# A decoder layer's first normalised rows: norm weights spread over 128 rows, squares and tile splits moved between engines

## The reference

```
h = rms_norm(x, ffn1_norm);  x = x + 0.5 * ((silu(h @ w1) * (h @ w3)) @ w2)
h = rms_norm(x, mix_norm);   x = x + concat(attention(h), ssd(h)) @ w_out
h = rms_norm(x, ffn2_norm);  x = x + 0.5 * ((silu(h @ w1) * (h @ w3)) @ w2)
out = rms_norm(x, final_norm)

rms_norm(x, w) = x * rsqrt(mean(x * x, last axis) + 1e-6) * w
```

## Time and profile before

| | us |
|---|---|
| three runs | 558.83, 558.90, 559.13; median 558.9 |
| the profiled execution | 558.88 |
| its span, first to last instruction | 557.1 |
| TensorE busy | 542.9 (97%) |
| VectorE busy | 436.1 (78%) |
| ScalarE busy | 333.2 (60%) |
| GpSimd busy | 63.9 (11%) |

### The profile page before, as it was taken

One profiled execution on the slowest core, in us unless ns is written; L12 is line 12 of the kernel. 1 busy time (PEld: TensorE's weight loads), 2 busy tenths in 40 slices (PEclk: granted clock), 3 DMA queues, 4 the chain that ended last, 5 costly groups with the idle time before them and its releaser, 6 DMA issues.

```text
span 557.1 us, 9770 instructions
## 1 busy us (share of the span) xinstructions
PE 542.9 (97%) x3670; PEld 494.9 (89%) x3670; DVE 436.1 (78%) x659; ACT 333.2 (60%) x539; POOL 63.9 (11%) x97
## 2 busy tenths in 40 slices
PE   8999999999999989999999999999999999999994
PEld 5999899999999879998889678889999999999993
DVE  4899898888887884877766666589898988888845
ACT  6757566555654565857675874376566556556533
POOL 2003000000000420512431002000000000000015
PEclk9999999999999999999999999999999999999998
DMA  9867955545664357555324235345575566655302
GB/s 269 291 227 233 322 190 189 167 175 186 226 226 151 91 158 229 167 188 176 128 78 151 75 82 167 131 154 169 198 251 201 178 208 226 226 161 182 108 1 75
DMA packets 69359, 97.65 MB, mean 175 GB/s; under 512 B 1862, under 2 KB 55298, under 8 KB 69331
## 3 DMA queue, kind: packets, MB, share of 16 engines
q1 hardware_dynamic: 68336, 94.55, 52.1%
q0 software_dynamic: 848, 2.47, 1.5%
q10 hardware_dynamic: 146, 0.27, 0.1%
HBM read 96.23 MB, written 1.05 MB: 175 GB/s over the span
## 4 chain that ended last, share of the span: by engine, by line
PE 81%; DVE 8%; ACT 3%; DMA 3%; issue 2%; POOL 1%; SPq 0%; POOLq 0%; DVEq 0%; ACTq 0%
PE bank L1575 25%; PE bank L1577 25%; PE bank L1576 25%; DMA raw<-in_ffn_w 3%; DVE w_lo L1048 2%; PE bank L1716 1%; ACT decay L924 1%; DVE x L1065 1%; ACT w_hi L602 1%; POOL rstd L472 1%; PE bank L1881 1%; PE bank L1882 1%; PE bank L1868 1%; DVE normed L1457 1%; PE bank L1880 0%
## 5 line engine op out<-in xcount | busy, mean ns | idle before, releaser
L1575 PE MATMUL bank<-hT_hi,w_hi 128*128 128x256 f32 x736 | 208.7, 284 | 0.2 <-DVE tok_rows L1216 0.2
L1576 PE MATMUL bank<-hT_lo,w_hi 128*128 128x256 f32 x736 | 208.0, 283 | 0.0
L1577 PE MATMUL bank<-hT_hi,w_lo 128*128 128x256 f32 x736 | 208.0, 283 | 0.0
L1048 DVE TENSOR_TENSOR w_lo<-raw,w_hi 128x1024 fp32r<-128x1024 f32 x128 | 158.4, 1240 | 28.5 <-ACT w_hi L602 28.0
L602 ACT ACTIVATE w_hi<-raw 128x1024 fp32r<-128x1024 f32 x128 | 134.1, 1055 | 43.4 <-PE bank L1577 24.7
L1575 PEld LDWEIGHTS bank<-hT_hi,w_hi 128*128 128x128 f32 x736 | 140.8, 191 | 3.3 <-DVE tok_rows L1216 1.4
L1576 PEld LDWEIGHTS bank<-hT_lo,w_hi 128*128 128x128 f32 x736 | 140.8, 191 | 1.6
L1577 PEld LDWEIGHTS bank<-hT_hi,w_lo 128*128 128x128 f32 x736 | 140.9, 191 | 0.0
L1575 PE MATMUL bank<-w_hi,hT_hi 128*128 128x512 f32 (+1 forms) x192 | 70.1, 365 | 2.0 <-DVE w_lo L1082 1.0
L1577 PE MATMUL bank<-w_hi,hT_lo 128*128 128x512 f32 (+1 forms) x192 | 68.1, 355 | 0.0
L1576 PE MATMUL bank<-w_lo,hT_hi 128*128 128x512 f32 (+1 forms) x192 | 68.0, 354 | 0.0
(11 more groups left out here) (217 smaller groups left out, 810.4 us busy)
## 6 DMA issues: line engine op xcount, KB each, us to landing
raw<-in_ffn_w SPq DMA_DIRECT2D x54, 1024.0 KB, 5.4
raw<-in_w_in SPq DMA_DIRECT2D x16, 1024.0 KB, 5.5
tok_rows<-in_ffn_w SPq DMA_DIRECT2D x10, 1024.0 KB, 5.3
raw<-in_w_out SPq DMA_DIRECT2D x6, 1024.0 KB, 4.9
raw<-in_ffn_w SPq DMA_DIRECT2D x8, 256.0 KB, 5.3
x<-in_x SPq DMA_DIRECT2D x4, 256.0 KB, 3.9
out_x<-normed SPq DMA_DIRECT2D x3, 256.0 KB, 2.3
norm_w<-in_mix_norm POOLq DMA_DIRECT2D x1, 512.0 KB, 5.4
```

The source lines that it names most:

```text
L1048: dve.tensor_tensor(lo, src, hi, ALU.subtract).then_inc(half_ready, 1)
L1575: pe.matmul(dst, lhs[0], rhs[0], start=start, stop=False, skip_group_check=True)
L1576: pe.matmul(dst, lhs[0], rhs[1], start=False, stop=False, skip_group_check=True)
L1577: return pe.matmul(dst, lhs[1], rhs[0], start=False, stop=stop, skip_group_check=True)
```

## The change

The identity's load moves from SP's queue to ScalarE's, ahead of the norm load. `norm_rows` and `ones_rows` take the place of the single rows: 128 partitions, of which all but the first are zero. VectorE clears `norm_rows` (128x1024), and ScalarE's load of the norm weights waits for that (`rows_cleared`). GpSimd clears the 128x128 of ones and then sets its first row. There are three warm-up matmuls instead of two. Of the first row tile ScalarE squares the left half and VectorE the right half, by a multiply with a reduction that also adds EPS; GpSimd adds the two and takes the power. ScalarE scales the left half before it rounds the first weights, and weight roundings stand between the two copies of the transposed banks. VectorE makes all low parts of the first tiles; GpSimd's subtraction and `low_ready` are gone. The diff's core:

```diff
-        norm_row = norm_w[0:1, 0, :]
-        ones_row = mix_w[0:1, D:D + P]
+        norm_rows = norm_w[:, 0, :]
+        ones_rows = mix_w[:, D:D + P]
...
# SP
-            sp.dma_start(cst[:, C_ID:C_ID + P], consts[:, C_ID:C_ID + P]).then_inc(ident_loaded, 16)
...
# GpSimd
-            pool.memset(ones_row, 1.0).then_inc(ones_ready, 1)
+            step(pool.memset(ones_rows, 0.0))
+            pool.memset(ones_rows[0:1, :], 1.0).then_inc(ones_ready, 1)
...
-                pool.wait_ge(mean_ready, 2 * n + t + 1)
+                pool.wait_ge(mean_ready, 2 * n + t)
...
-            row_rstd(0, 0)
-
-            slot = ffn_half(0, 0, 0, 0)[1]
-            pool.wait_ge(hi_ready, 1)
-            pool.tensor_tensor(rows_part(w_lo[:, slot, :], 1), rows_src(0, 0, 1),
-                               rows_part(w_hi[:, slot, :].bitcast(f32), 1), ALU.subtract).then_inc(low_ready, 1)
+            pool.wait_ge(sq_ready, 2)
+            pool.tensor_tensor(mean_sq[:, 0:1], sumsq[:, 0, 0:1], sumsq[:, 1, 0:1], ALU.add).then_inc(left_mean_ready, 1)
+            pool.wait_ge(left_mean_ready, 1)
+            pool.tensor_tensor(rstd[:, 0:1], mean_sq[:, 0:1], minus_half[:, :], ALU.pow).then_inc(rstd_ready, 1)
             row_rstd(0, 1)
...
# ScalarE
-            act.dma_start(norm_row, norms[0].rearrange("(a d) -> a d", a=1)).then_inc(norm_loaded[0], 16)
-            for c in range(2):
-                act.wait_ge(x_loaded[c], 16)
-                square_x(0, 0, c)
+            act.dma_start(cst[:, C_ID:C_ID + P], consts[:, C_ID:C_ID + P]).then_inc(ident_loaded, 16)
+            act.wait_ge(rows_cleared, 1)
+            act.dma_start(norm_rows[0:1, :], norms[0].rearrange("(a d) -> a d", a=1)).then_inc(norm_loaded[0], 16)
+            act.wait_ge(x_loaded[0], 16)
+            square_x(0, 0, 0)
+            first_scale(0, 0)
             rows_hi(0, 0, 0)
-            first_scale(0, 0)
+            hT_hi_part(1, T_BANKS[0], 0, 0)
             rows_hi(0, 1, 0)
-            norm_hi(0, 0)
+            hT_hi_part(2, T_BANKS[1], 4, 0)
             rows_hi(0, 0, 1)
             rows_hi(0, 1, 1)
...
# VectorE
-            for c in range(2):
-                dve.wait_ge(x_loaded[c], 16)
+            right = slice(512, 1024)
+            dve.memset(norm_rows, 0.0).then_inc(rows_cleared, 1)
+            dve.wait_ge(x_loaded[1], 16)
+            dve.tensor_tensor_reduce(z_silu[:, 0, right], x[:, 0, right], x[:, 0, right], 1.0 / D, EPS,
+                                     ALU.mult, ALU.add, sumsq[:, 1, 0:1]).then_inc(sq_ready, 1)
+            dve.wait_ge(x_loaded[0], 16)
             first_weigh(0, 0)
-            rows_lo(0, 0, 0).then_inc(top_ready, 1)
             dve.wait_ge(norm_spread, 2)
             dve.wait_ge(rstd_ready, 1)
-            right = slice(512, 1024)
             dve.scalar_tensor_tensor(normed[:, 0, right], x[:, 0, right], rstd[:, 0:1], bank[:, 3, :],
                                      ALU.mult, ALU.mult).then_inc(scaled_right, 1)
+            rows_lo(0, 0, 0).then_inc(top_ready, 1)
+            hT_lo_part(1, T_BANKS[0], 0, 0)
             rows_lo(0, 1, 0).then_inc(top_ready, 1)
-            norm_lo(0, 0)
-            dve.wait_ge(low_ready, 1)
-            rows_lo(0, 1, 1).then_inc(half_ready, 2)
+            hT_lo_part(2, T_BANKS[1], 4, 0)
+            for kind in range(2):
+                rows_lo(0, kind, 1).then_inc(half_ready, 1)
...
# TensorE
-                for _ in range(2):
+                for _ in range(3):
                     pe.matmul(bank[:, U_BANK, 0:P], zeros, zeros, start=True, stop=True)
...
-                    pe.matmul(bank[:, 2 + c, :], ones_row, norm_row[:, c * 512:(c + 1) * 512],
+                    pe.matmul(bank[:, 2 + c, :], ones_rows, norm_rows[:, c * 512:(c + 1) * 512],
```

More of the change, by code:

```diff
@@ L194, in build @@
         top_ready = sem("top_ready")
-        low_ready = sem("low_ready")
         zeros_ready = sem("zeros_ready")
         ones_ready = sem("ones_ready")
+        rows_cleared = sem("rows_cleared")
         norm_spread = sem("norm_spread")
```

## The result

The changed kernel took 560.89 us (median of 7, 559.38 to 563.11) against 559.23 for the kernel before (median of 7, 558.83 to 559.67): ratio 1.0031, 95% interval 1.0018 to 1.0044. It is slower by about 1.7 us. A second series gave the same ratio: 560.63 (11 times, 559.28 to 564.62), 1.0031 (1.0015 to 1.0048). A ratio compares all times of a kernel with those of the kernel before in the same series, so it need not be that of the medians. The forecast was 558.5, with a range up to 560.0. The times of the changed kernel also spread more.

A forecast was written before the change was run, and what follows sets the result against it. It took one serial chain at the start, from the first weights' landing to TensorE's resumption at 12.92, to bound what changes; +0.23 and -0.60 gave -0.37, so 558.88 became 558.5 us, range 557.6 to 560.0.

The forecast's parts named there:

- When the norm row lands: ScalarE's norm load, issued at 1.97 behind the clearing, lands 1.9 later, at 3.9; bounds 3.6 and 5.0.
- X: Start of TensorE's first pass spreading the norm row over the partitions: 2.35 before, forecast 3.9.
- Clock: TensorE's rise from 1.2 to 2.4 GHz, placed at 7.4 if full-row passes count although 127 rows are zero.
- the lead of 3.5: Time in us from the start of full-row work on TensorE to its clock's rise, as seen before.
- H: TensorE's resumption of its first product, once both lower halves are there: 12.92 before, forecast 12.55.
- a clock that does not rise sooner: Rival, chance 0.28: zero rows do not lift TensorE's clock; H at 13.55, +0.65, 559.5 us.
- Sum: At H: +0.23 for the later second copy, -0.60 from second copy to H, together -0.37 us.
- The norm row lands late: Rival, chance 0.12: the load travels among others, each us costs one; 559.6 us if it lands at 5.0.
- a tail of 0.12: Chance of slower from the clock rival with the norm row landing past 4.4, passing +1.1 us.
- The weighing: VectorE's scaling by the spread norm weights, starting 2.19 after the first pass; left half 6.1 to 6.8.
- the splits' 0.6 us: Reordered roundings and VectorE's subtractions: second copy to H takes 2.82 instead of 3.42.
- The root: Reciprocal root from shared squares and GpSimd's power, ready at about 5.9 against 5.77, hidden before the left scaling at 6.85.

The follow-up runs named there:

- late_one_row: Changed kernel with clearing, wait and late norm load kept, but the spread reads one row again: 561.16 us, ratio 1.0037 to the kernel before.
- fill_gap: Changed kernel with eight warm-up matmuls of zeros in place of three: 560.03 us, ratio 1.0023 to the kernel before.
- one_row: Changed kernel with the one-row spread, early norm load, no clearing and two warm-up matmuls of before: 558.99 us, ratio 0.9996 to the kernel before.
- ident_sp: Changed kernel with the identity's load back in SP's queue: 559.91 us, ratio 1.0015 to the kernel before.
- row_copy: Changed kernel with the norm row loaded at once into another row and copied by VectorE into the cleared rows: 558.56 us, ratio 0.9986 to the kernel before.
- row_copy_sp: row_copy with the identity's load on SP's queue and one identity matmul instead of two before the transposes: 558.45 us, ratio 0.9987 to the kernel before.
- row_copy_full: row_copy_sp with four warm-up matmuls in place of three: 558.35 us, ratio 0.9988 to the kernel before.

## Why the prediction was wrong, point by point

**When the norm row lands: mis-sized, the main fault.** The forecast put X at 3.9, 1.9 behind the issue at 1.97, inside bounds of 3.6 and 5.0. In six traces of the changed kernel it is 4.87 to 5.33, median 5.05: 2.9 to 3.4 behind the issue. The other kernels with this load gave 4.00 to 5.99. Even the upper bound, the identity's 3.0, was passed in four of the six. The forecast leaned to the lower bound because the load is small and has its own queue; its one packet began 2.0 to 2.7 behind the issue all the same, where it was 0.92 before. That step is 1.15 us too small.

**Clock: right mechanism, optimistic size.** The rise did come sooner because of the zero rows (late_one_row, fill_gap). But the lead of 3.5, read from one trace, is the short end. The first trace had it, and the third was near (3.8). In the other four the identity matmuls were still at the low clock and the rise fell among the transposes, at 9.9 to 10.5, so near 5 behind X; with the identity on SP's queue it came late among the transposes or just behind them, 5.5 to 6.1 behind X. H - X was forecast as 8.65 and is 9.15 in the median of six: 0.5 us. The rival's price for a clock that does not rise sooner, 9.65, was met to 0.01 by late_one_row and one_row, and that is partly luck: it was meant for 128-row passes, where ident_sp measured 9.36.

**Sum.** -0.37 + 1.15 + 0.5 = +1.3, of the 1.7 measured. The rest, 0.4, lies behind H: in the median of the six traces H is 14.14, 1.2 later than before, and the execution is H plus 546.3, where it was 546.0. Over all traces that second part goes from 545.9 to 547.2, and once to 548.2, so 0.4 is within its spread. Whether the change has a part in it is open, since the kernel before has only one trace.

**The rivals.** "The norm row lands late" is what happened, with the price given (one us each); its chance of 0.12 was far too low. And it does not come alone: a later start of the full-row work and a slower rise add up. The forecast put the two together only in a tail of 0.12, and its range ended at 560.0.

**What held.** The third warm-up was hidden. The clearing ended at 1.94 as said and the norm load went out at 1.97, but by luck: the memset took 0.91 in place of 1.21 and began at 1.02 in place of 0.73, and the two misses cancel. The weighing followed the first pass by 2.16, and where the clock was up the first copy followed the transposes by 0.64. H followed the second copy by 2.85 (forecast 2.82, before 3.42): the splits' 0.6 us was won. The root came at 6.23 instead of 5.9, since the right half of x landed at 4.53 (4.05 before, 4.2 in the forecast), and it was hidden. That half landed at 4.5 to 4.8 in every trace with the identity in ScalarE's queue and at 4.0 to 4.5 with it in SP's. The shift passed on one for one up to 46.96.

**The new wait's real price.** The load left its cover: issued at 0.73 it met a nearly idle DMA system and was in use 1.62 later; issued at 1.97 it lies among 0.5 MB of rows and the first weights. That the traffic is what holds it back fits the busy share (0.90 against 0.29) and the wait of its packet; no run took the traffic away. The wait for the clearing was 1.2 us and cost 2.7 (2.35 to 5.05).

## What to carry to other kernels

A small load on the critical path is cheapest as the very first; before putting a wait in front of it, price its landing among the traffic that will then be running, as a spread and not as a number. If data must be prepared around it, load it early to another place and move it with an engine, as row_copy does. To lift TensorE's clock use matmuls on all rows; zeros do it, one-row matmuls did not. A gap between them and the real work probably costs part of the effect, and none of it pays while the real work waits for a late load: fill_gap's median stayed above that of the kernel before (1.0023).

## What was unexpected of the hardware

- All-zero matmuls on 128 rows lifted the clock from 1.2 to 2.4 GHz (spread passes at half length at 4.84 behind 3.6 us of zeros, in two of four traces; in the third within the spread, in the fourth not before the zeros ended at 4.9), while 3.75 us of dense one-row passes did not (before, one_row, late_one_row).
- A gap of 0.2 to 0.4 us behind the warm-up went with a rise only at 7.4 to 7.6 (row_copy, row_copy_sp) in place of about 5.4, within the spread (row_copy_full); one trace each.
- One 4 KB load, issued at 1.97 in every trace that has it there, was in use 2.0 to 4.0 us later. Its single packet moved in 0.16 us and spent the rest of the time mostly waiting to start.
- Four 128-row passes at the low clock took 1.15 behind one-row passes and 0.85 behind 128-row passes (late_one_row, changed kernel).
- A VectorE memset of 128x1024 float32 took 0.91 us, less than a two-operand operation of that size (1.21).
